# Two projection tiles of the first layer accumulated row by row together, with the inverse norms kept in SBUF

## The reference, cut to what matters

```python
h = rms_norm(x, norm_g[i]) * (1.0 + scale[:, None]) + shift[:, None]
hc = rms_norm(xc, norm_g[i]) * (1.0 + scale_c) + shift_c
...
def rms_norm(x, g):
    xf = x.astype(jnp.float32)
    y = xf * lax.rsqrt(jnp.mean(xf * xf, axis=-1, keepdims=True) + NORM_EPS)
    return (y * g.astype(jnp.float32)).astype(x.dtype)
...
q, k, v, g = jnp.split(h @ w_in, [GQA_WIDTH, GQA_WIDTH + GQA_KV_WIDTH, GQA_WIDTH + 2 * GQA_KV_WIDTH], axis=-1)
```

## Time and profile before

| what | value |
|---|---|
| median of 3 runs | 1547.32 us (1546.25 to 1550.59) |
| the profiled execution's own time | 1546.84 us |
| its span, first to last instruction | 1545.1 us |
| PE busy | 1495.9 us, 97% of the span |
| DVE busy | 1003.6 us, 65% |
| ACT busy | 811.1 us, 52% |
| POOL busy | 419.4 us, 27% |

### The profile page before, as it was taken

One profiled execution on the slowest core, in us unless ns is written; L12 is line 12 of the kernel. 1 busy time (PEld: TensorE's weight loads), 2 busy tenths in 40 slices (PEclk: granted clock), 3 DMA queues, 4 the chain that ended last, 5 costly groups with the idle time before them and its releaser, 6 DMA issues. The chain is left out here.

```text
span 1545.1 us, 26314 instructions
## 1 busy us (share of the span) xinstructions
PE 1495.9 (97%) x9467; PEld 1310.5 (85%) x9467; DVE 1003.6 (65%) x2139; ACT 811.1 (52%) x1848; POOL 419.4 (27%) x513
## 2 busy tenths in 40 slices
PE   6999999999999999989999999999998999999998
PEld 3788788897898898978888888889997889899996
DVE  5665645428888888864348966576221887787883
ACT  7422321128777777754554333444111887777772
POOL 2322101002222111100012333221390454554541
PEclk9899999999999999999999999999998999999999
DMA  9435425409111244023224454478957999999882
GB/s 358 161 122 157 129 83 178 159 18 274 24 25 24 81 157 143 7 88 116 82 89 127 131 166 139 132 219 268 288 142 216 301 297 272 257 264 274 260 232 68
DMA packets 195653, 252.23 MB, mean 163 GB/s; under 512 B 32978, under 2 KB 157476, under 8 KB 195492
## 3 DMA queue, kind: packets, MB, share of 16 engines
q1 hardware_dynamic: 193076, 242.16, 51.5%
q10 hardware_dynamic: 2448, 8.39, 1.9%
HBM read 187.59 MB, written 78.76 MB: 172 GB/s over the span
## 5 line engine op out<-in xcount | busy, mean ns | idle before, releaser
L1195 ACT ACTIVATE prob<-S,nm,qk_inv 128x512 f32<-128x512 f32 (+1 forms) x208 | 146.3, 707 | 3.5 <-DVE nm L1131 3.5
L600 PE MATMUL pp<-h_hi,w_hi 128*128 128x512 f32 (+1 forms) x408 | 147.6, 362 | 0.0
L2593 DVE CUSTOM_DVE_ANT_0 nprob<-nS,bias_set 128x640 f32<-128x640 f32 x128 | 105.0, 821 | 61.6 <-PE nS L2425 40.5
L601 PE MATMUL pp<-h_lo,w_hi 128*128 128x512 f32 (+1 forms) x408 | 144.6, 354 | 0.0
L602 PE MATMUL pp<-h_hi,w_lo 128*128 128x512 f32 (+1 forms) x408 | 144.5, 354 | 0.0
L2511 ACT CAST npt_hi<-nTB 128x256 fp32r<-128x256 f32 (+1 forms) x256 | 103.7, 425 | 61.2 <-PE nTB L2436 54.5
L1149 DVE TENSOR_TENSOR ptlo<-TB,pthi 128x512 fp32r<-128x512 f32 (+1 forms) x192 | 114.5, 596 | 29.8 <-ACT pthi L1207 28.0
L1207 ACT CAST pthi<-TB 128x512 fp32r<-128x512 f32 (+1 forms) x192 | 99.3, 517 | 63.1 <-PE TB L1076 62.4
L1124 DVE TENSOR_REDUCE mx<-S 128x1 f32<-128x512 f32 (+1 forms) x208 | 116.5, 579 | 10.7 <-PE S L1068 9.4
L2608 DVE TENSOR_TENSOR npt_lo<-nTB,npt_hi 128x256 fp32r<-128x256 f32 (+1 forms) x256 | 115.2, 482 | 2.8 <-ACT npt_hi L2511 1.5
L2502 ACT ACTIVATE nprob<-nprob,selector 128x640 f32<-128x640 f32 x128 | 106.5, 832 | 10.7 <-DVE selector L2593 10.0
(11 more groups left out here) (328 smaller groups left out, 4481.2 us busy)
## 6 DMA issues: line engine op xcount, KB each, us to landing
kq_scratch<-p_stage SPq DMA_DIRECT2D x96, 256.0 KB, 3.9
keys<-kq_scratch SPq DMA_DIRECT2D x32, 768.0 KB, 5.1
bias_set<-bias_scratch SPq DMA_DIRECT2D x64, 384.0 KB, 6.3
v_strip<-v_scratch SPq DMA_DIRECT2D x128, 128.0 KB, 5.2
wearly<-in_mod_w SPq DMA_DIRECT2D x15, 1024.0 KB, 7.5
bias_scratch<-bias_wide_scratch SPq DMA_DIRECT2D x16, 768.0 KB, 10.8
w_raw<-in_na_w_in SPq DMA_DIRECT2D x11, 1024.0 KB, 6.0
wside<-in_mod_w SPq DMA_DIRECT2D x9, 1024.0 KB, 7.2
```

What stands on the lines that cost most here:

```text
L600: pe.matmul(acc, whi[:, k, ws], hi[:, k, a:a + width], start=(k == 0), stop=False)
L601: pe.matmul(acc, whi[:, k, ws], lo[:, k, a:a + width], start=False, stop=False)
L1195: act.activation(prob[:, p % 5, a:a + n], S[:, score_bank(p, k), 0:n], ACT.Exp, bias=nm[:, p % 5:p % 5 + 1], scale=q_scale(h - 1, p) if p ...
```

## The change

Row k of tile 1 is now accumulated among the rows of tile 0, one to three rows behind. For that the banks 3 to 5 must be free early: ACT copies the inverse norms to SBUF (`kept`, in the place where the rotary tables lie later), and every `normalise` but the first reads them there. The first reads two banks from PSUM in pieces, and the copy for the context tokens. The second weight block is loaded and split earlier; the tables are loaded later. Rows 0 to 2 of tile 0, and row 0 of tile 1, go among the last products and turns of the vectors. The squares of tile 0 are added within tile 2.

```diff
--- before.py
+++ after.py
@@ -162,10 +162,11 @@
     PARTS = [(0, NCTX, 1), (NCTX, NLAT, 0)]
     BY_POOL = (3, 5, 7)
 
-    def __init__(self, c, consts, l, xt, hi, lo, mod, sums, t_, rb):
+    def __init__(self, c, consts, l, xt, hi, lo, mod, sums, t_, rb, kept):
 
         self.consts, self.l, self.xt, self.hi, self.lo, self.mod, self.sums = consts, l, xt, hi, lo, mod, sums
-        self.t_, self.rb = t_, rb
+        self.t_, self.rb, self.kept = t_, rb, kept
+        self.keptd, self.pieces = c.sem(f"inverses_kept{l}"), c.sem(f"first_row_pieces{l}")
         self.root, self.inv = c.sb(f"root{l}", [P, TT]), c.sb(f"inv{l}", [P, TT])
         self.summed, self.rooted, self.recd, self.spread = (
             c.sem(f"{x}{l}") for x in ("summed", "rooted", "recip_done", "inv_spread"))
@@ -189,10 +190,25 @@
                                 self.inv[:, t:t + 1].broadcast_to([P, P]), self.consts["ident"][:, :])
         last.then_inc(self.spread, 1)
 
+    def keep_inverses(self, act):
+
+        act.wait_ge(self.spread, 1)
+        act.copy(self.kept[:, 0:NCTX], self.rb[:, 0, 512 - NCTX:512]).then_inc(self.keptd, 1)
+        for i, bank in enumerate((2, 1)):
+            act.wait_ge(self.pieces, i + 1)
+            act.copy(self.kept[:, NCTX + 512 * (bank - 1):NCTX + 512 * bank], self.rb[:, bank, :]).then_inc(self.keptd, 1)
+
     def normalise(self, dve, k):
 
-        inverses = self.rb.rearrange("p a n -> p (a n)")[:, 512 - NCTX:512 - NCTX + T]
-        dve.tensor_tensor(self.xt[:, k, :], self.xt[:, k, :], inverses, ALU.mult).then_inc(self.normed, 1)
+        if k:
+            dve.wait_ge(self.keptd, 3)
+            dve.tensor_tensor(self.xt[:, k, :], self.xt[:, k, :], self.kept[:, :], ALU.mult).then_inc(self.normed, 1)
+            return
+        for bank in (2, 1):
+            cols = slice(NCTX + 512 * (bank - 1), NCTX + 512 * bank)
+            dve.tensor_tensor(self.xt[:, 0, cols], self.xt[:, 0, cols], self.rb[:, bank, :], ALU.mult).then_inc(self.pieces, 1)
+        dve.wait_ge(self.keptd, 1)
+        dve.tensor_tensor(self.xt[:, 0, 0:NCTX], self.xt[:, 0, 0:NCTX], self.kept[:, 0:NCTX], ALU.mult).then_inc(self.normed, 1)
 
     def high(self, act, vectors, k):
         if k % 4 == 0:
@@ -427,6 +443,8 @@
             t_ = c.sb("scaled", [P, 4, T])
         with c.place((120, 130)):
             sq = c.sb("x_squares", [P, D])
+        with c.place(AREA_TABLES):
+            kept = c.sb("inverses", [P, T])
         with c.place((140, 150)):
             side1, side_sum0 = c.sb("wside_1", [P, 4, 512]), c.sb("side_sum0", [P, 512])
         with c.place((40, 80), (148, 156), (192, 200)):
@@ -436,7 +454,7 @@
         with c.place((200, 203.5)):
             vec, vec2, x_sums = c.sb("vec_rows", [P, P]), c.sb("vec_rows2", [P, P]), c.sb("x_sums", [P, TT])
             ps, sums, rb = c.ps("pp", [P, RING, 512]), c.ps("qk_sums", [P, 512]), c.ps("k_inv_spread", [P, 512])
-            norm = NormSteps(c, consts, 0, xt, hi, lo, mod, x_sums[:, :], t_, ps[:, 3:6, :])
+            norm = NormSteps(c, consts, 0, xt, hi, lo, mod, x_sums[:, :], t_, ps[:, 3:6, :], kept)
             side_sum1 = c.sb("side_sum1", [P, 512])
         tps, small = ps[:, 0:2, :], ps[:, 2, :]
         vectors = SideVectors(c, io, consts, "a", mod, cols, [sums, rb], early_rows, early + [side1],
@@ -492,10 +510,10 @@
                     src = io["ctx"][0, t * P:(t + 1) * P] if t < CT else io["x"][0, (t - CT) * P:(t - CT + 1) * P]
                     sp.dma_start(xin[:, t, :], src).then_inc(s_x[t], 16)
                 for g in range(2 * len(vectors.halves)):
-                    if g == 4:
-                        first.load(sp, 0)
+                    if g in (4, 6):
+                        first.load(sp, g // 2 - 2)
                     vectors.load(sp, g)
-                first.load(sp, 1)
+                sp.wait_ge(norm.normed, KT)
                 sp.dma_start(cos[:, :], io["cos"][:, NCTX:]).then_inc(tabs, 16)
                 sp.dma_start(sin[:, :], io["sin"][:, NCTX:]).then_inc(tabs, 16)
 
@@ -565,42 +583,54 @@
                 vectors.product(pe, 2)
                 vectors.product(pe, 3)
                 vectors.turn(pe, 1)
-                for u in range(2, 4):
-                    vectors.product(pe, 2 * u)
-                    vectors.product(pe, 2 * u + 1)
-                    vectors.turn(pe, u)
-
-                def first_tile():
-                    pe.wait_ge(first.wlo, 1)
-                    for b in range(2):
-                        pe.wait_ge(taken[b], TT)
-                    for k in range(KT):
-                        pe.wait_ge(norm.los, 2 * k + 2)
-                        for stat, mov in ((whi, hi), (whi, lo), (wlo, hi)):
-                            for j, (a, width) in enumerate(ALL_CHUNKS):
-                                last = pe.matmul(ps[:, j, 0:width], stat[:, k, 0:P], mov[:, k, a:a + width],
-                                                 start=(k == 0 and mov is hi and stat is whi),
-                                                 stop=(k == KT - 1 and stat is wlo))
-                    last.then_inc(mm, 1)
+
+                def row(n, k):
+                    if k == 0:
+                        pe.wait_ge(first.wlo, n + 1)
+                        for b in range(2):
+                            pe.wait_ge(taken[b], TT)
+                        if n:
+                            pe.wait_ge(norm.keptd, 3)
+                    pe.wait_ge(norm.los, 2 * k + 2)
+                    ws = slice(n * P, n * P + P)
+                    for stat, mov in ((whi, hi), (whi, lo), (wlo, hi)):
+                        for j, (a, width) in enumerate(ALL_CHUNKS):
+                            last = pe.matmul(ps[:, 3 * n + j, 0:width], stat[:, k, ws], mov[:, k, a:a + width],
+                                             start=(k == 0 and mov is hi and stat is whi),
+                                             stop=(k == KT - 1 and stat is wlo))
+                    if k == KT - 1:
+                        last.then_inc(mm, 1)
+
+                vectors.product(pe, 4)
+                vectors.product(pe, 5)
+                row(0, 0)
+                vectors.turn(pe, 2)
+                row(0, 1)
+                vectors.product(pe, 6)
+                row(1, 0)
+                vectors.product(pe, 7)
+                row(0, 2)
+                vectors.turn(pe, 3)
+                for n, k in ((1, 1), (0, 3), (1, 2), (0, 4), (1, 3), (0, 5), (1, 4), (0, 6), (0, 7), (1, 5), (1, 6), (1, 7)):
+                    row(n, k)
 
                 def tile(n):
                     s = n % 2
                     ws = slice(s * P, (s + 1) * P)
-                    if n == 1:
-                        pe.wait_ge(first.wlo, 2)
+                    pe.wait_ge(w_lo, n - 1)
+                    if n - 2 < NQK:
+                        pe.wait_ge(squared, n - 1)
                     else:
-                        pe.wait_ge(w_lo, n - 1)
-                        if n - 2 < NQK:
-                            pe.wait_ge(squared, n - 1)
-                        else:
-                            pe.wait_ge(g_out, n - 1 - NQK)
+                        pe.wait_ge(g_out, n - 1 - NQK)
                     for j, (a, width) in enumerate(ALL_CHUNKS):
                         acc = ps[:, 3 * s + j, 0:width]
                         for k in range(KT):
                             pe.matmul(acc, whi[:, k, ws], hi[:, k, a:a + width], start=(k == 0), stop=False)
                             pe.matmul(acc, whi[:, k, ws], lo[:, k, a:a + width], start=False, stop=False)
                             last = pe.matmul(acc, wlo[:, k, ws], hi[:, k, a:a + width], start=False, stop=(k == KT - 1))
-                        if j == (0 if n == NQK else 1) and 1 <= n <= NQK:
+                        if j == 0 and n == 2:
+                            add_squares(0)
+                        if j == (0 if n == NQK else 1) and 2 <= n <= NQK:
                             add_squares(n - 1)
                         if j == 0 and n >= 3 and n % 2 and n // 2 - 1 < BESIDE:
                             beside.fold(pe, n // 2 - 1)
@@ -643,8 +673,7 @@
                                             inv[:, QH + h, t:t + 1].broadcast_to([P, P]), consts["ident"][:, :])
                     last.then_inc(spread, 1)
 
-                first_tile()
-                for n in range(1, N):
+                for n in range(2, N):
                     tile(n)
                 pe.wait_ge(vw_lo, 1)
                 for t in range(TT):
@@ -707,6 +736,7 @@
                 act.wait_ge(squared_x, TT)
                 act.sem_inc(norm.summed, 1)
                 norm.roots(act)
+                norm.keep_inverses(act)
                 for k in range(3):
                     norm.scale_on_act(act, vectors, k)
                 for k in range(3):
@@ -856,9 +886,9 @@
                 pool.wait_ge(cst, 3)
                 first.split(pool, 0)
                 norm.scale_on_pool(pool, vectors, 3)
```

(2 more changed lines are left out.)

## The result

| | us |
|---|---|
| kernel before, median of 20 runs beside the changed one | 1548.83 (1544.64 to 1554.11) |
| kernel after, median of 20 runs | 1552.97 (1549.40 to 1558.38) |
| ratio after / before | 1.0029, 95% interval 1.0019 to 1.0038 |
| span of the profiled execution after | 1551.9 |

The change makes the kernel slower, by about 4.1 us (1552.97 - 1548.83). The prediction was 1545.8 us, with a range to 1548.6, a gain of 1.5 us against the kernel before; so it was wrong in sign.

A forecast was written before the change was run, and what follows sets the result against it. PE, busy 97% of the span, was taken as the bound; tile 1 ending at 74.3 instead of 75.77 us gained 1.5 us, which taken from the median 1547.32 gave 1545.8 us, range 1542.2 to 1548.6.

The forecast's parts named there:

- the head: Stretch up to the end of tile 1: forecast to end at 74.3 instead of 75.77 us, 1.5 us gained.
- the 54.7 at which it would decide: Latest end of PE's turn 3, in us, as 21.1 us of rows follow it; the rival where it comes later had 0.09.
- the 46 us assumed: Time at which PE's full clock was taken to return, with PE steadily at work from 40.0 us.
- theory A: Likeliest case, chance 0.70: DVE and POOL alternate, tile 1 ends 1.5 us earlier, 1545.8 us; by clock alone 1543.5 to 1547.6.
- the half clock at the first row of tile 0: Starting observation in the kernel before: tile 0's first row on PE takes 3.15 us at half clock, other rows 1.76.
- the turns: In DVE's norm products and low parts: POOL and DVE instructions with both operands in SBUF alternate whole; lows end at 63.2, not 59.43.
- more than 2 us beside POOL's splits: Sign that the likeliest case is right: DVE's `normalise` instructions take over 2 us while POOL's splits run.
- rival D: Tile 3's weights on DVE: if their chain of 10.3 us exceeds 11.9, PE waits; 3 us more gives 1547.3; chance 0.06.
- Behind it PE goes on in both kernels with the same work, at full clock, and I let a gain or loss here pass on whole.: After the end of tile 1: the 1.5 us gained there was assumed to reach the whole time undiminished.
- Behind tile 1: Check of tiles 2 and 3: tile 2 does not wait, tile 3 finds its weights with 1.6 us to spare.
- same: Whole-kernel outcome within about 0.3% (4.6 us), which a measurement cannot tell from no change; chance 0.87.

## Why the prediction was wrong

**Right: the head.** The first row was forecast at 40.0 and came at 39.33; the low parts end at 61.92 (63.2); turn 3 begins at 51.53 and ends at 52.1 (53.2), far from the 54.7 at which it would decide; the clock returned earlier than the 46 us assumed, within the first row (its products take 1.41, 1.27 and 1.01, the next row's 0.85). So tile 1 ended earlier than forecast: the gain was 2.6 us, not 1.5, near the 73 that the prediction's theory A gives for full clock from 40. Two terms were off by size, in the same direction. Other executions narrow this: without the last stage tile 2 starts at 73.34 or 73.91 in the new order and at 76.07 or 76.29 in the old, a gain of 1.3 to 2.1 us once the 0.85 for the squares is taken off. And the half clock at the first row of tile 0, from which the prediction starts, belongs to its one trace: in four other profiled executions of the old order that row's first group takes 0.83 to 0.84 us, not 1.41, and tile 2 starts at 76.07 to 76.79 all the same, since the rows wait 1.4 to 1.8 us for DVE's low parts instead.

**Half right: the turns.** That POOL and DVE take turns where DVE has both operands in SBUF shows beside both splits. The vectors' columns paid for it as forecast (unit 1 is done at 35.97, forecast 36.3; unit 2 at 46.68, forecast 46.9), but the `normalise` did not. DVE and POOL after, beside each other (compare):

```profile
28.61 2.89 DVE L205 TENSOR_TENSOR xt<-xt,inverses 128x1280 f32<-128x1280 f32 x2
...
32.02 1.72 DVE L205 TENSOR_TENSOR xt<-xt,inverses 128x1280 f32<-128x1280 f32 x1
...
33.88 2.09 DVE L335 TENSOR_TENSOR mod<-mod,cols 128x8 f32<-128x8 f32 x1
...
44.26 2.42 DVE L341 SCALAR_TENSOR_TENSOR mod<-mod,cols 128x4 f32<-128x4 f32 x2
```

```profile
32.48 3.47 POOL L278 TENSOR_TENSOR w_lo<-w_raw,w_hi 128x1024 fp32r<-128x1024 f32 x1
36.05 7.17 POOL L246 TENSOR_SCALAR scaled<-xt,mod 128x256 f32<-128x256 f32 x2
...
44.29 2.37 POOL L278 TENSOR_TENSOR w_lo<-w_raw,w_hi 128x1024 fp32r<-128x1024 f32 x1
```

The `normalise` of two SBUF operands take 1.45 us each, and 1.72 where one starts just ahead of a subtraction, so "more than 2 us beside POOL's splits" was wrong. The small columns are held to the end of a subtraction, 2.09 in place of 0.17, and 2.42 in place of the 0.23 of the earlier trace rows. POOL's subtraction takes 3.47 in place of 2.38 and its two parts of a scaled copy 7.17 in place of 3.77, while DVE issues one instruction behind another. The section of the Trainium skill that the prediction quotes ("SBUF — State Buffer", "Who interferes with whom") says that the later one blocks until the other has ended; the columns agree, with 2.09 us, and so does the first subtraction, which starts at 32.48, behind the `normalise` of 32.02, and takes the 3.47. In the half it was DVE again that paid, 2.14 us for POOL's product of 2.40. Which of the two pays in each place the prediction did not work out.

**Right as far as it went: rival D.** Tile 3 starts at 88.91, its weights are done at 87.20 (85.98 + 1.22): 1.7 us to spare, against 1.6 forecast.

**Wrong: "Behind it PE goes on in both kernels with the same work, at full clock, and I let a gain or loss here pass on whole."** This is the step that failed; the part "Behind tile 1" was to check it. There I followed the squares of tile 0 to the low weights of tile 3, because PE waits for these next, and stopped. On DVE the half sum stands right behind those weights, and its reader, the fold, comes on PE only 24 products into tile 3. Its cover of 7.6 us was in the trace of before and was never worked out. The later squares took 5.8 of it, PE's own lead 2.4, POOL's product beside the half 2.1. With this term the sum is -2.6 + 2.8, or about nothing, as at tile 4 of the profiled execution; the low clock behind the stand adds 2.75 us in the trace where it falls for longest, and the timed runs without the last stage show +3.3 altogether. Moving the fold by one chunk takes it out and gives -1.7 to -2.0 without the last stage, close to the -1.5 forecast: without this wait the forecast holds there, though in part by luck, as the head gained anything from 1.3 to 2.6 us from one execution to the next.

**The chances.** The loss of 0.27% to 0.29% lies just inside the bound of 0.3% that I gave to "same"; but the range ended at 1548.6, as no rival held a wait behind tile 3.

**Open.** How often the clock falls behind the fold (in two of three profiled executions of that kernel), since filling the stand did not show in the time; and why a lead of 2.6 us at tile 4 is hardly seen in the whole kernel, whose last stage differs by 3 us between two executions of the same work (355.8 and 359.0).

## What to carry to other kernels

When a step is moved later, list everything that stands behind it in the queue of each engine it feeds, and follow each to its reader, not only to the first one that PE asks for; the cover to write down is the arrival of the reader minus the end of the writer, and a lead of the reader uses it up as well. A change that speeds up the bounding engine and delays an engine at its side spends the same cover twice. Where the one trace and the timed runs disagree on a few microseconds, cut the program behind the stage in question: that brought the spread of the runs from 9 us to between 0.6 and 3.4.

## What the runs showed of the hardware

- The same stand of PE, 2.82 to 2.83 us in three traces, was followed by a granted clock of 1.00 in one execution, of 0.57 for 4 us in another and of 0.51 for 6 us in the third. In the third it cost 2.82 us and 2.75 more, twice its length; the profile of the first hides that.
- POOL was stretched by DVE instructions with their operands in SBUF as well as the other way round: the two parts of a scaled copy that took 7.17 us together took 3.75 once four of DVE's products read PSUM, as before the change (3.77).
- 24 products of PE taken out of the kernel before, 5.4 us, gained nothing: a wait of 4.8 us for ACT took their place.
